# The sums over tiles of four norms, made by TensorE tile by tile in a two-block transformer kernel

## What is computed

```python
def rms_norm(x, g):
    xf = x.astype(jnp.float32)
    y = xf * lax.rsqrt(jnp.mean(xf * xf, axis=-1, keepdims=True) + EPS)
    return y.astype(x.dtype) * g

# first block, layer l: ffn, mixer (even: attention and mLSTM; odd: GLA), ffn
x = x + 0.5 * mx[:, 2] * swiglu(ada_norm(x, norm_g[l, 0], mx[:, 0], mx[:, 1]), ...)
x = x + mx[:, 5] * mixer(ada_norm(x, norm_g[l, 1], mx[:, 3], mx[:, 4]))
x = x + 0.5 * mx[:, 8] * swiglu(ada_norm(x, norm_g[l, 2], mx[:, 6], mx[:, 7]), ...)
...
return rms_norm(x, final_g)

# second block, layer i: a mixer (MLA, then neighbourhood attention), then an MLP
x = _layer_norm(alpha * x + g1 * y, ln1_g[i], ln1_b[i])
x = _layer_norm(alpha * x + g2 * _mlp(x * (1 + sc2) + sh2, mlp_w1[i], mlp_w2[i]), ln2_g[i], ln2_b[i])
```

## Time and profile before

| what | value |
|---|---|
| median of 3 runs | 3345.33 us (3344.7 to 3346.12) |
| profiled execution | 3346.43 us |
| its span, first to last instruction | 3344.4 us |
| mean granted clock of PE | 0.924 of 2.4 GHz |
| PE busy | 2954.9 us (88%) |
| DVE busy | 1955.4 us (58%) |
| ACT busy | 1185.1 us (35%) |
| POOL busy | 564.3 us (17%) |

### The profile page before, as it was taken

The page is one execution under the profiler, slowest core; times in us unless marked ns, Lnnn a source line. Parts: engine busy times, 40 slices in busy tenths (PEclk is TensorE's granted clock), DMA queues, the critical chain, the costliest instruction groups (busy, mean ns, idle before and its releaser), DMA issues.

```text
span 3344.4 us, 38315 instructions
## 1 busy us (share of the span) xinstructions
PE 2954.9 (88%) x15158; PEld 2402.1 (72%) x15158; DVE 1955.4 (58%) x3186; ACT 1185.1 (35%) x1946; POOL 564.3 (17%) x583
## 2 busy tenths in 40 slices
PE   0999999677899999999996689989979999888797
PEld 0788887433788888888794589965677778864797
DVE  6888752456577866778543456543356564433554
ACT  2322232343332224222334435434352223525452
POOL 1000010121200001000101011013341113126431
PEclk9999999766899999999997589999989999889898
DMA  6455522100255544555341035521124442232453
GB/s 232 164 201 202 182 81 95 44 0 0 89 195 195 207 145 139 195 201 199 102 139 32 0 101 184 182 70 38 48 77 148 162 152 97 100 86 22 133 180 111
DMA packets 125281, 412.13 MB, mean 123 GB/s; under 512 B 25088, under 2 KB 27136, under 8 KB 124464
## 3 DMA queue, kind: packets, MB, share of 16 engines
q1 hardware_dynamic: 107824, 346.78, 31.1%
q0 software_dynamic: 17280, 62.92, 5.5%
HBM read 408.60 MB, written 1.05 MB: 122 GB/s over the span
## 4 chain that ended last, share of the span: by engine, by line
PE 78%; DVE 9%; ACT 7%; issue 3%; POOL 2%; DMA 1%; SPq 0%; POOLq 0%; ACTq 0%; DVEq 0%
PE bank L1966 24%; PE bank L1968 23%; PE bank L1967 23%; PE bank L2143 2%; DVE sb_temp L1542 1%; POOL sb_temp L1025 1%; DVE sb_rstd L1584 1%; PE bank L2274 1%; PE bank L2104 1%; PE bank L2221 1%; DVE sb_split_low L1528 1%; PE bank L2273 1%; DVE sb_temp L1592 1%; PE bank L2133 1%; ACT sb_temp L1455 1%
## 5 line engine op out<-in xcount | busy, mean ns | idle before, releaser
L1966 PE MATMUL bank<-sb_h_high,sb_split_high 128*128 128x256 f32 (+1 forms) x3048 | 1060.1, 348 | 123.3 <-DVE sb_h_low L1598 79.6
L1967 PE MATMUL bank<-sb_h_low,sb_split_high 128*128 128x256 f32 (+1 forms) x3048 | 1041.4, 342 | 0.0
L1968 PE MATMUL bank<-sb_h_high,sb_split_low 128*128 128x256 f32 (+1 forms) x3048 | 1040.6, 341 | 0.0
L1528 DVE TENSOR_TENSOR sb_split_low<-sb_raw,sb_split_high 128x1024 fp32r<-128x1024 f32 x515 | 636.4, 1242 | 277.0 <-ACT sb_split_high L1157 272.9
L1966 PEld LDWEIGHTS bank<-sb_h_high,sb_split_high 128*128 128x128 f32 x3048 | 591.3, 194 | 209.1 <-issue 85.5
L1157 ACT ACTIVATE sb_split_high<-sb_raw 128x1024 fp32r<-128x1024 f32 x515 | 535.2, 1051 | 391.7 <-DMA sb_raw<-weights 391.7
L1967 PEld LDWEIGHTS bank<-sb_h_low,sb_split_high 128*128 128x128 f32 x3048 | 594.0, 195 | 67.7 <-issue 0.5
L1968 PEld LDWEIGHTS bank<-sb_h_high,sb_split_low 128*128 128x128 f32 x3048 | 592.8, 194 | 66.8
L1542 DVE CUSTOM_DVE_ANT_0 sb_temp<-sb_ada_ffn,sb_cond_ffn 128x1024 bf16<-128x1024 f32 x408 | 479.1, 1219 | 29.3 <-DMA sb_ada_ffn<-ada 29.0
L1648 DVE SCALAR_TENSOR_TENSOR sb_x_res<-bank,sb_gates,sb_x_res 128x256 f32<-128x256 f32 x272 | 122.3, 478 | 297.5 <-PE bank L1968 297.1
L1966 PE MATMUL bank<-sb_hidden_high_ffn,sb_split_high 128*128 128x512 f32 (+1 forms) x788 | 272.8, 346 | 0.0
(11 more groups left out here) (240 smaller groups left out, 3335.9 us busy)
## 6 DMA issues: line engine op xcount, KB each, us to landing
sb_raw<-weights SPq DMA_DIRECT2D x515, 512.0 KB, 3.3
sb_ada_ffn<-ada SPq DMA_DIRECT2D x102, 512.0 KB, 4.3
sb_ada_ffn<-ada POOLq DMA_DIRECT2D x102, 512.0 KB, 3.6
sb_ada_mlp<-ada SPq DMA_DIRECT2D x18, 512.0 KB, 4.2
sb_ada_mlp<-ada POOLq DMA_DIRECT2D x18, 512.0 KB, 4.5
sb_cond_ffn<-cond SPq DMA_DIRECT2D x3, 1024.0 KB, 5.3
sb_na_raw<-na_rpb SPq DMA_DIRECT2D x32, 96.0 KB, 5.8
sb_x_res<-tokens SPq DMA_DIRECT2D x1, 2048.0 KB, 14.0
```

The source lines that it names most:

```text
L1528: do.tensor_tensor(m.low[i][:, :], m.raw[i][:, :], m.high[i][:, :].bitcast(F32), ALU.subtract).then_inc(*dve.mark("split_low", s))
L1966: do.matmul(out, ah, bh, start=start and j == 0, stop=False)
L1967: do.matmul(out, ah, bl, start=False, stop=False)
L1968: last = do.matmul(out, al, bh, start=False, stop=stop and j == len(terms) - 1)
```

## The change

At the four norms n12, final, ln10 and ln11 POOL adds nothing any more. PE takes each tile as it comes, a product with the ones of 256 columns, and the eight products of a sum add up in bank 7 (`start` at the first, `stop` at the last). The product of tile k - 1 stands behind the ordinary products of tile k. In the step `centre` the products of squares 0 to 6 are issued at once, and square 7 with the step `sum`. ACT waits for PE's product k - 2 before it writes square k, where it waited for POOL's addition. All other norms are as before.

```diff
+ALONE = ("n12", "final", "ln10", "ln11")
...
     def square(tag, k, p):
+        if tag in ALONE:
+            return
         pool.wait_ge("squared", (tag, k, p))
...
     def add_mean(tag, k, p):
+        if tag in ALONE:
+            return
         wait_for_x(pool, LAYER_NORMS[tag][0], k, p)
...
     def squared(tag, k, p):
 
-        if k >= 2:
+        if k >= 2 and tag in ALONE:
+            act.wait_ge("summed", ("square", tag, k - 2, p))
+        elif k >= 2:
             act.wait_ge("added", ("square", tag, max(k - 2, 1), p))
...
+    def add_up(src, k, p, *keys):
+
+        if k == 0:
+            free(6 + p)
+        do.matmul(m.bank[6 + p][:, 0:NC_TOK], m.C("ones"), src[:, COLS[p]], start=k == 0, stop=k == DT - 1).then_inc(
+            *pe.mark("summed", *keys))
...
+    def add_square(tag, k, p):
+        pe.wait_ge("squared", (tag, k, p))
+        add_up(m.squares[k % 2], k, p, ("square", tag, k, p), (tag, p))
+
+    def square(tag, k, p):
+        if tag in ALONE and k:
+            add_square(tag, k - 1, p)
+
+    def centre(tag, p):
+        if tag in ALONE:
+            for k in range(DT - 1):
+                add_square(tag, k, p)
 
     def sum_of_squares(tag, p):
         pe.wait_ge("inputs", "all")
-        pe.wait_ge("added", ("square", tag, DT - 1, p))
-        add_up(tag, p, (tag, p))
+        if tag in ALONE:
+            add_square(tag, DT - 1, p)
+        else:
+            pe.wait_ge("added", ("square", tag, DT - 1, p))
+            add_all(p, (tag, p))
         read[6 + p] = "mean", (tag, p)
 
+    def add_x(tag, k, p):
+        wait_for_x(pe, LAYER_NORMS[tag][0], k, p)
+        add_up(m.x[:, k, :], k, p, ("mean", tag, p))
+
+    def add_mean(tag, k, p):
+        if tag in ALONE and k:
+            add_x(tag, k - 1, p)
+
     def mean_sum(tag, p):
-        pe.wait_ge("added", ("x", tag, DT - 1, p))
-        add_up(tag, p, ("mean", tag, p))
+        if tag in ALONE:
+            add_x(tag, DT - 1, p)
+        else:
+            pe.wait_ge("added", ("x", tag, DT - 1, p))
+            add_all(p, ("mean", tag, p))
         read[6 + p] = "centred", (tag, DT - 1, p)
```

More of the change, by code:

```diff
@@ L1980, in h_product, with add_all @@
             (("h_low", (tag, k, p) if p in H_PARTS.get(tag, (0, 1)) else (tag, k)), *columns_of(s % SLOTS, k), *m.h_term(k, p)) for k in range(DT)])
-    def add_up(tag, p, key):
-        bank = 6 + p
-        free(bank)
-        do.matmul(m.bank[bank][:, 0:NC_TOK], m.C("ones"), m.acc[:, COLS[p]], start=True, stop=True).then_inc(*pe.mark("summed", key))
+    def add_up(src, k, p, *keys):
[3 more added lines that the diff above has]
+            *pe.mark("summed", *keys))
+    def add_all(p, key):
+        free(6 + p)
+        do.matmul(m.bank[6 + p][:, 0:NC_TOK], m.C("ones"), m.acc[:, COLS[p]], start=True, stop=True).then_inc(*pe.mark("summed", key))
+    def add_square(tag, k, p):
[8 more added lines that the diff above has]
+                add_square(tag, k, p)
     def sum_of_squares(tag, p):
         pe.wait_ge("inputs", "all")
-        pe.wait_ge("added", ("square", tag, DT - 1, p))
-        add_up(tag, p, (tag, p))
-        read[6 + p] = "mean", (tag, p)
-    def mean_sum(tag, p):
-        pe.wait_ge("added", ("x", tag, DT - 1, p))
-        add_up(tag, p, ("mean", tag, p))
+        if tag in ALONE:
[3 more added lines that the diff above has]
+            add_all(p, (tag, p))
+        read[6 + p] = "mean", (tag, p)
+    def add_x(tag, k, p):
[4 more added lines that the diff above has]
+            add_x(tag, k - 1, p)
+    def mean_sum(tag, p):
+        if tag in ALONE:
[3 more added lines that the diff above has]
+            add_all(p, ("mean", tag, p))
         read[6 + p] = "centred", (tag, DT - 1, p)
@@ L2286, in na_scores @@
         read[u % 3] = "na_lat", u
-    work = {"sum": sum_of_squares, "mean_sum": mean_sum, "small_square": small_square, "up": up, "down": down, "fm": fm,
+    work = {"sum": sum_of_squares, "square": square, "add_mean": add_mean, "centre": centre, "mean_sum": mean_sum, "small_square": small_square, "up": up, "down": down, "fm": fm,
             "out": out, "tm": tm, "forget_sums": forget_sums, "rope": rope, "da_scores": da_scores, "da_turn": da_turn,
```

## The result

The kernel before and the changed one ran in turn on one chip, eleven executions of each. Their medians are 3345.8 us and 3356.58 us (3348.77 to 3357.94); the ratio of the two kernels' times is **1.0022, 95% interval 1.0014 to 1.003**, that is 7.4 us more (4.7 to 10). The forecast was 6.1 us more, 3351.4 us, with a range from 3348.6 to 3354.3. The median of 3356.58 lies above this range; the ratio on the 3345.33 us from which the forecast started gives 3352.7, inside it. The interval of the ratio holds the forecast of 6.1 us and two of its rivals (7.5 and 8.8) alike; only the steps tell them apart.

The account below looks back on a forecast made before the run. TensorE (PE) was taken to bound the kernel, never waiting in the four streams. The terms 10.6 - 3.98 - 0.6 + 0.1 = +6.1 us on 3345.33 gave 3351.4 us, range 3348.6 to 3354.3.

Parts of the forecast that it names:

- two of its rivals (7.5 and 8.8): Clock falls before the first square product, staying down through one chain (+7.5) or both (+8.8); chance 0.33 together.
- part 1: Four streams before n12, final, ln10, ln11: 25 added products cost PE 0.425 us each, 10.6 us lost.
- The one product behind final: Among final's seven added products, one falls behind its stream and counts in full, 0.42 us, since PE runs on.
- part 2: POOL's last addition leaves the path: 1.27 us gained at n12, 1.91 at ln10, 0.80 at ln11, 3.98 in all.
- part 3: Sums of squares at ln10 and ln11: first product waits for all centrings; 0.3 us gained at each, 0.6 together.
- The ring: Squares at ln10 and ln11: two buffers pace product and square, 1.21 us per two tiles at full clock, 1.73 at half.
- The term that was mis-sized: Squares at ln10 and ln11: three or four tiles at half clock, last product ending at about 8.7 us.
- The rival with one chain at half clock (+7.5): One chain of squares at half loses 1.07 us, the other gains 0.3; chance 0.33, shared with both chains at half.
- The table load: At ln10, ScalarE's 1.28 us load behind the last square, formerly under POOL's additions, may show by 0.1 us.
- Streams that absorb the products: Weights set the streams' pace, so 25 products cost nothing: 3338.5 us, chance 0.03; with the clock falling 3340.8, chance 0.04.
- the wait for the bank: At ln10 and ln11 the first square product waits for all eight centrings of the mean, not starting before 2.79 us.

Follow-up runs that it names:

- e10: The changed kernel with each product inside the four streams (tiles 0 to 5) made twice, 24 products more; ratio 1.0063 to the kernel before.
- e4: The change made only at ln10 and ln11, with n12 and final as in the kernel before; ratio 1.0006 to the kernel before.
- e6: The changed kernel with seven unused products filling PE's gap before the first square product at ln10 and ln11; ratio 1.0018 to the kernel before.
- e7: The changed kernel, but at the four norms' first sums POOL adds tiles 0 to 6 and PE takes the last; ratio 0.9987 to the kernel before.
- e5: The changed kernel with the squares of ln10 and ln11 summed in bank 6, the mean staying in bank 7; ratio 1.0006 to the kernel before.
- e8: The changed kernel with POOL adding tiles 0 to 6 of first sums and ln10, ln11 squares in bank 6; 3335.76 us, ratio 0.9966 to the kernel before.
- e11: e8 run again unchanged; median 3333.8 us, ratio 0.9966 to the kernel before.
- e3: The change made only at n12 and final, with ln10 and ln11 as in the kernel before; ratio 1.0008 to the kernel before.

## Why the prediction was nearly right, and where not

- **In-stream products, step part 1: right.** 0.425 us each was taken from one place in the trace. The streams of n12, final, ln10 and ln11 give 0.41, 0.42, 0.44 and 0.44, and e10's second ones 0.44 to 0.46; the paces told of in the last section blur this by some 0.03 at n12. 25 of them were to cost 10.6; measured are 10.2 in the streams and 0.14 behind final, 10.4 us. The one product behind final was to cost 0.42 and shows 0.14 in this trace, but the stretch it lies in varies by 0.3 to 0.6 us between traces that have the same instructions there. Over all traces it comes out: the ten that have one product more there take 30.62 us on the average, the four that don't 30.18, 0.44 apart.
- **POOL's last addition, part 2: right at n12 (1.27 of 1.27) and ln11 (0.79 of 0.80), too high at ln10 (1.65 of 1.91).** The step of the prediction that failed here asked when PE would be done, and not what DVE does in between. Behind x DVE has a `split_low` of 1.22 us in its queue (3125.07 in the rows above). PE's last product of x, started at 3125.21, is over at 3125.91 (3124.47 + 1.44), but the first centring starts at 3126.20 with no idle time before it: DVE's own instruction is last there now. At n12 DVE has the same split behind x, but the square lies between and covers it. On the other hand POOL's addition made this wait 3.18 us in the first trace of before and 3.51 in the third, so 1.65 is at the low end of what goes. At n12 it made the wait 2.99 to 3.01 us in three traces and 3.51 in e4, so that the exact 1.27 is partly luck.
- **The chain of squares, part 3: the mechanism right, the size and the sign wrong.** The first square product stands right behind the last centring (0.15 us), 2.88 us behind the first (forecast 2.79). The ring takes 1.26 us a pair at full clock (forecast 1.21; e6's chain at full clock takes 7.82 us to DVE's reading, 7.78 to the end of the last product, forecast 7.55) and 1.8 at half (forecast 1.73). The term that was mis-sized is the end of the last product, 8.7 us behind the first centring, with 0.3 us gained at each place. Measured are 0.75 us lost at ln10 and 0.12 at ln11, 1.47 us away from the forecast in all, and this is nearly all of the difference between 6.1 and 7.5. About 0.8 of it is the share at half clock at ln10: the clock stood at half from 3127.7, over a microsecond before the first square product, to 3134.5, so six of the eight products ran at half where three or four had been taken (1.95 us by e6, where the forecast has 8.7 - 7.55 = 1.15). At ln11 it stood there from 3339.3 to 3342.7, which the first two products and the last two escaped: four products, as forecast, but they cost 1.32 us in place of 1.15. The remaining 0.5 are hand-offs, 0.23 at each place at full clock. The rival with one chain at half clock (+7.5) meets the sum better than the forecast does, partly by luck: its terms are 1.07 lost and 0.3 gained, and neither was measured. Nor is the size fixed by the code: with the same chain e7 lost 0.11 at ln10 and gained 0.23 at ln11. The table load (1.28 us at 3135.20, ended at 3136.48) holds up the square root at ln10 by 0.1 as forecast (the mean ends at 3135.97 + 0.42); it lies behind the steps of the table and is not in their 7.5.
- **Streams that absorb the products** (the rival on the other side) are excluded by the earlier trace rows, the rows of after, and e10.
- **What the prediction didn't see** is that its own finding, the wait for the bank, was the most expensive thing in the change next to the products in the streams (10.4 us). It took the wait as given and priced the ring behind it. e5 shows that an idle bank was at hand, worth 7.1 us in both chains together (6.1 from e7 to e8).

The sum: 10.4 - 3.7 + 0.87 = 7.5 us, forecast 10.6 - 3.98 - 0.6 + 0.1 = 6.1. The mechanism held in parts 1 and 3, and in part 2 but for the split behind ln10; of the misses, -0.2 in part 1 and +0.3 in part 2 offset each other in part, and part 3 is what remains.

## What to carry to other kernels

When a sum is moved from a waiting helper engine to the engine that bounds the kernel, only the last tile belongs there: products in a stream that never waits cost their full time (25 x 0.42 us here), while the idle engine adds the early tiles for nothing. When a chain of small products stands behind a wait, ask which buffer or bank the first of them shares with a reader that isn't done; the wait here cost once as delay (1.9 us) and once more as half clock (1.3 to 1.95 us in the changed kernel). And before a wait is said to go, look at what the waiting engine itself has queued in front of the next step.

## What the runs showed of the hardware

**Back-to-back products run at one of three paces.** With PE never waiting and the granted clock at 1.00, the starts of the products of 256 columns lie 117.3 ns apart on the average in some stretches, 118.7 ns in others and, more rarely, 120.0 ns. The window from 2000 to 2100 us, PE only, in the traces of e8 and then of e11, the same program (PE busy and records, granted clock, DMA share, GB/s):

```profile
2000.00:2100.00 100.00, 100.00 (x845) 1.00 0.55 185
```

```profile
2000.00:2100.00 100.00, 100.00 (x854) 1.00 0.57 185
```

845 records in one and 854 in the other, 1.1% apart, at the same clock. The pace holds for tens of microseconds and more. It isn't the kernel's: e8 and e11 are one program, and n12's stream in three traces of the kernel before took 17.09, 17.09 and 16.89 us. From n12's mean to the first tiles of ffn11's down projection this is worth 1.5 us (148.7 us in the three traces of before, 147.2 in the changed kernel, but 148.6 and 147.2 in e8 and e11). The third pace is the 0.9 us in e3's last stream: seven tiles of 11.5 us there, of 11.4 in the kernel before, over 75 us of ln11's stream in before and in e3:

```profile
3245.00:3320.00 75.00, 75.00 (x634) 1.00 0.44 148
```

```profile
3255.00:3330.00 75.00, 75.00 (x627) 1.00 0.44 143
```

At 120.0 in place of 118.7 ns the 687 starts from tile 0 to tile 7 take 0.9 us more. What sets it no run here shows. A change worth a microsecond can't be read from spans; it has to be read from steps around it.

**Two executions of one program differ by 3 us in one attention stage** (19.0 and 22.2 us), with the granted clock at half for 20 us in the one and 27 in the other. In a chain of eight products behind an idle stretch of PE the same code took 8.79 to 9.81 us, by where the half clock came to lie.
